# Attention and activation transposes on TensorE as pairs of bf16 in one 4-byte element

## What is computed

```
h = x @ W_in + b_in            -> q (1024) | k (256) | v (256) | z (2048) | gate_a (1024) | gate_g (1024)
y_a = attention(q, k, v, sinks) @ W_branch_attn     # 16 query heads, 4 key heads, head size 64, window 128
y_g = (u * (tril(W_s) LN(v') + b_s)) @ W_branch_gmlp, u | v' = gelu(z), chunks of 128 positions
mix = sigmoid(gate_a) * y_a + sigmoid(gate_g) * y_g
x1  = LayerNorm(alpha * x + mix @ W_out)
out = LayerNorm(alpha * x1 + relu(x1 @ W_up)^2 @ W_down)      # W_up 1024 x 4096
```

## Time and profile before

| | us |
|---|---|
| median of 3 runs (range) | 1052.94 (1052.09 to 1054.36) |
| the profiled execution, its own time | 1046.84 |
| its span, first to last instruction, slowest core | 1045.3 |
| TensorE busy in it | 1023.3 (98%) |
| DVE busy | 611.5 (59%) |
| ACT busy | 360.4 (34%) |
| POOL busy | 89.1 (9%) |

### The profile page before, as it was taken

One profiled execution on the slowest core, in us unless ns is written; L12 is line 12 of the kernel. 1 busy time (PEld: TensorE's weight loads), 2 busy tenths in 40 slices (PEclk: granted clock), 3 DMA queues, 4 the chain that ended last, 5 costly groups with the idle time before them and its releaser, 6 DMA issues.

```text
span 1045.3 us, 16998 instructions; the slowest of 8 cores (1043.9 to 1045.3 us)
## 1 busy us (share of the span) xinstructions
PE 1023.3 (98%) x6054; PEld 498.9 (48%) x6054; DVE 611.5 (59%) x1087; ACT 360.4 (34%) x484; POOL 89.1 (9%) x152
## 2 busy tenths in 40 slices
PE   8999999999999999999999999999999999999994
PEld 3446455554444444444444645555444444444442
DVE  2866477765876312336787827777486832133476
ACT  0454666651425200330024646666123430023100
POOL 4210000000111000000012000000010100010000
PEclk9999999999999999999999999999999999999998
DMA  9995234241797812953198222542156464086011
GB/s 160 188 174 95 41 53 98 54 102 33 150 162 150 142 20 35 166 82 82 61 185 149 50 41 44 91 102 51 61 124 138 75 129 80 1 134 108 21 61 80
DMA packets 20484, 98.65 MB, mean 94 GB/s; under 512 B 2353, under 2 KB 2993, under 8 KB 11954
## 3 DMA queue, kind: packets, MB, share of 16 engines
q0 software_dynamic: 13344, 73.41, 42.1%
q1 hardware_dynamic: 7058, 24.16, 6.8%
HBM read 162.57 MB, written 8.39 MB: 164 GB/s over the span
## 4 chain that ended last, share of the span: by engine, by line
PE 93%; DVE 3%; DMA 1%; issue 1%; ACT 1%; POOL 0%; DVEq 0%; POOLq 0%; ACTq 0%
PE ps L431 61%; PE ps L1147 20%; PE ps L924 3%; PE ps L674 2%; PE ps L942 2%; PE ps L889 2%; DMA ring<-wz 1%; PE ps L795 1%; DVE scr L392 1%; PE ps L972 1%; PE ps L1063 1%; PE ps L742 1%; DVE scr L897 0%; ACT scr L409 0%; DVE Cg L392 0%
## 5 line engine op out<-in xcount | busy, mean ns | idle before, releaser
L431 PE MATMUL ps<-reg,ring 128*128 128x512 bf16 x1536 | 344.7, 379 | 0.0
L431 PE MATMUL ps<-xT_s,ring 128*128 128x512 bf16 x1120 | 252.2, 375 | 0.2 <-DVE reg L392 0.2
L431 PEld LDWEIGHTS ps<-reg,ring 128*128 128x128 bf16 x1536 | 147.6, 98 | 172.7 <-issue 2.1
L1147 PE MATMUL ps<-ring,reg 128*128 128x512 bf16 x992 | 214.8, 379 | 0.0
L403 ACT ACTIVATE scr<-ps 128x512 f32<-128x512 f32 x128 | 76.4, 597 | 263.4 <-PE ps L431 260.0
L431 PEld LDWEIGHTS ps<-xT_s,ring 128*128 128x128 bf16 x1120 | 104.0, 98 | 115.0 <-issue 4.5
L392 DVE SCALAR_TENSOR_TENSOR reg<-ps,scr 128x512 bf16<-128x512 f32 x128 | 87.7, 690 | 113.8 <-ACT scr L403 113.7
L1147 PEld LDWEIGHTS ps<-ring,reg 128*128 128x128 bf16 x992 | 97.1, 98 | 117.0
L897 DVE CUSTOM_DVE_ANT_1 scr<-ps,masks 128x1024 f32<-128x1024 f32 x64 | 78.1, 1220 | 42.8 <-PE ps L889 34.9
L403 ACT ACTIVATE scr<-scr,amx 128x1024 bf16<-128x1024 f32 x64 | 73.2, 1144 | 15.9 <-DVE amx L392 11.8
L459 POOL DMA_DIRECT2D ring<-wst x62 | 34.6, 561 | 456.8 <-PE ps L431 165.2
(11 more groups left out here) (85 smaller groups left out, 722.7 us busy)
## 6 DMA issues: line engine op xcount, KB each, us to landing
ring<-wst POOLq DMA_DIRECT2D x62, 1024.0 KB, 10.7
regK<-x SPq DMA_DIRECT2D x16, 512.0 KB, 6.7
y<-scr SPq DMA_DIRECT2D x15, 512.0 KB, 2.6
lnbuf<-lnrep SPq DMA_DIRECT2D x4, 1024.0 KB
xT_s<-xt POOLq DMA_DIRECT2D x2, 1024.0 KB, 22.4
ring<-wz POOLq DMA_DIRECT2D x2, 1024.0 KB, 10.1
xT_s<-xt POOLq DMA_DIRECT2D x7, 256.0 KB, 19.3
ring<-wz POOLq DMA_DIRECT2D x7, 256.0 KB, 16.0
```

The costliest lines, as they stand in the source:

```text
L431: r = e.matmul(out, lhsT=a, rhs=b, start=(k == 0), stop=(k == 7))
L1147: r = e.matmul(ps[:, b2 + half, :], lhsT=hreg[fi // 8][:, th, fi % 8, bb * 128:(bb + 1) * 128], rhs=wd[quarter][:, fi % 4, half * 512:(hal ...
```

## The change

At all three places two bf16 neighbours are read as one float32, so that a row of 256 bf16 is 128 elements and one 128 x 128 transpose moves what two did: 4 transposes in place of 8, with a float32 identity. The bits pass through unchanged; in PSUM the two bf16 of a pair lie next to each other. The copy out of PSUM now reads every second bf16 and writes them side by side.

- Attention probabilities: Exp writes key s of half c at place 2s + c, so that the pair is (key s, key 128 + s), and the copy has the same order (j, c, q) in `pts` as before.
- Attention output and x1: the pair is two neighbouring features, 2p and 2p + 1, so partition p of the even block holds feature 2p of 256. The host orders the rows of W_branch_attn and W_up to match (`pairs`); their loads have the same shape and size.
- The identity is loaded straight into its own float32 buffer; its cast goes. The planner's figure for a transpose group is 0.23 in place of 0.45; that for Exp is written as 1.2 (1.19 by the helper's rule). The figures for the copies are as before.

```diff
-        identb = sb("identb", [128, 128], BF16)
+        ident = sb("ident32", [128, 128])
...
-            ld(idf, ident_d[:, :], [B_idf], after)
+            ld(ident[:], ident_d[:, :], [C["ident"]], after)
...
-            cp(identb[:], idf, [B_idf], [C["ident"]])
...
-                act(p16, ms, AF.Exp, bms + [B_amx[ai]], bpt, bias=mx[:, 4 + bb:5 + bb], scale=0.125)
+                act(p16.rearrange("p (j s c) -> p j c s", j=4, c=2), ms.rearrange("p (j c s) -> p j c s", j=4, c=2), AF.Exp, bms + [B_amx[ai]], bpt,
+                    bias=mx[:, 4 + bb:5 + bb], scale=0.125).cost = 1.2
...
                     for j in range(4):
                         pj = (j % 2) * 2 + j // 2
-                        for cc in range(2):
-                            r = e.transpose(out=PTp[:, j, cc, :], in_=c["p16"][:, pj * 256 + cc * 128:pj * 256 + (cc + 1) * 128], identity=identb[:])
+                        r = e.transpose(out=PT[:, j, :], in_=c["p32"][:, pj * 128:(pj + 1) * 128], identity=ident[:])
...
-                timed(P.op("pe", f, reads=c["bpt"] + [C["ident"]], writes=[B_ps[b]]), 0.45)
+                timed(P.op("pe", f, reads=c["bpt"] + [C["ident"]], writes=[B_ps[b]]), 0.23)
...
-                either(pts.bitcast(BF16), ps[:, b, :].bitcast(BF16), [B_ps[b]], bpts)
+                either(c["pts"], ps[:, b, :].bitcast(BF16).rearrange("p (j q c) -> p j c q", j=4, c=2), [B_ps[b]], bpts)
...
-                    for e2 in range(2):
-                        for b4 in range(4):
-                            r = e.transpose(out=AT[:, e2, b4 * 128:(b4 + 1) * 128], in_=ablk[:, bi, b4, e2 * 128:(e2 + 1) * 128], identity=identb[:])
+                    for b4 in range(4):
+                        r = e.transpose(out=ps[:, b, b4 * 128:(b4 + 1) * 128], in_=A32[:, b4 * 128:(b4 + 1) * 128], identity=ident[:])
...
-                either(attnT[:, th, 2 * hk:2 * hk + 2, :], AT, [B_ps[b]], [B_at[th]])
+                either(attnT[:, th, 2 * hk:2 * hk + 2, :], ps[:, b, :].bitcast(BF16).rearrange("p (t e) -> p e t", e=2), [B_ps[b]], [B_at[th]])
...
-                    for e_ in range(8):
-                        r = e.transpose(out=XT[:, e_, :], in_=xb[:, e_ * 128:(e_ + 1) * 128], identity=identb[:])
+                    for e2 in range(4):
+                        r = e.transpose(out=ps[:, b, e2 * 128:(e2 + 1) * 128], in_=xb[:, e2 * 128:(e2 + 1) * 128], identity=ident[:])
...
-                either(x1T[:, th, :, bb * 128:(bb + 1) * 128], XT, [B_ps[b]], [B_x1T[blk]])
+                either(x1T[:, th, :, bb * 128:(bb + 1) * 128].rearrange("p (f e) t -> p f e t", e=2),
+                       ps[:, b, :].bitcast(BF16).rearrange("p (f t e) -> p f e t", f=4, e=2), [B_ps[b]], [B_x1T[blk]])
...
+    def pairs(w):
+        return np.ascontiguousarray(np.transpose(w.reshape(-1, 128, 2, w.shape[1]), (0, 2, 1, 3)).reshape(w.shape))
+    w_up0, w_dn0, w_o0 = pairs(f(w_up)[0]), f(w_down)[0], f(w_out)[0]
+    wa0, wg0 = pairs(f(w_branch_attn)[0]), f(w_branch_gmlp)[0]
```

More of the change, by code:

```diff
@@ L557, in build_program @@
         ts(hgate[:], bcol[:, 16:32], 0.5, ALU.mult, [C["bcol"]], [C["hgate"]])
-        t01, t2, idf = r3f[:, 0:1024], r3f[:, 1024:1152], r3f[:, 1152:1280]
+        t01, t2 = r3f[:, 0:1024], r3f[:, 1024:1152]
         ones = r3f[:, 1280:1344].bitcast(BF16)
-        B_tri, B_idf = Buf("tri"), Buf("idf")
+        B_tri = Buf("tri")
         def load_consts(after):
@@ L808, in group @@
                 Prog.alias_after(B_ablk, [B_zero])
-                Prog.alias_after(B_at, [B_cst, B_tri, B_idf, C["ones"]])
+                Prog.alias_after(B_at, [B_cst, B_tri, C["ones"]])
             else:
@@ L904, in att_S @@
                 p16 = pt.bitcast(BF16)
-                act(p16, ms, AF.Exp, bms + [B_amx[ai]], bpt, bias=mx[:, 4 + bb:5 + bb], scale=0.125)
-                cx[t].update(p16=p16, bpt=bpt)
+                act(p16.rearrange("p (j s c) -> p j c s", j=4, c=2), ms.rearrange("p (j c s) -> p j c s", j=4, c=2), AF.Exp, bms + [B_amx[ai]], bpt,
+                    bias=mx[:, 4 + bb:5 + bb], scale=0.125).cost = 1.2
+                cx[t].update(p32=pt, bpt=bpt)
                 if bb == 3:
@@ L916, in att_T @@
                 b = 2 + rot("ptb", 2)
-                PTp = ps[:, b, :].bitcast(BF16).rearrange("p (j c q) -> p j c q", j=4, c=2)
+                PT = ps[:, b, :].rearrange("p (j q) -> p j q", j=4)
                 def f(e):
@@ L965, in att_A @@
                 b = 2 + rot("ptb", 2)
-                AT = ps[:, b, :].bitcast(BF16).rearrange("p (e q) -> p e q", e=2)
+                A32 = ablk[:, bi].rearrange("p b c -> p (b c)").bitcast(F32)
                 def f(e):
                     r = None
-                    for e2 in range(2):
-                        for b4 in range(4):
-                            r = e.transpose(out=AT[:, e2, b4 * 128:(b4 + 1) * 128], in_=ablk[:, bi, b4, e2 * 128:(e2 + 1) * 128], identity=identb[:])
-                    return r
-                timed(P.op("pe", f, reads=[B_ablk[bi], C["ident"]], writes=[B_ps[b]]), 0.45)
-                either(attnT[:, th, 2 * hk:2 * hk + 2, :], AT, [B_ps[b]], [B_at[th]])
+                    for b4 in range(4):
+                        r = e.transpose(out=ps[:, b, b4 * 128:(b4 + 1) * 128], in_=A32[:, b4 * 128:(b4 + 1) * 128], identity=ident[:])
+                    return r
+                timed(P.op("pe", f, reads=[B_ablk[bi], C["ident"]], writes=[B_ps[b]]), 0.23)
+                either(attnT[:, th, 2 * hk:2 * hk + 2, :], ps[:, b, :].bitcast(BF16).rearrange("p (t e) -> p e t", e=2), [B_ps[b]], [B_at[th]])
             SK = 5
@@ L1051, in o_K @@
                 either(xb.bitcast(BF16), x1[:, blk, :], [B_x1[blk]], bxb)
-                oc[blk] = (xb.bitcast(BF16), bxb)
+                oc[blk] = (xb, bxb)
             def o_C(blk):
@@ L1057, in o_C @@
                 b = bank()
-                XT = ps[:, b, :].bitcast(BF16).rearrange("p (e t) -> p e t", e=8)
                 def f(e):
                     r = None
-                    for e_ in range(8):
-                        r = e.transpose(out=XT[:, e_, :], in_=xb[:, e_ * 128:(e_ + 1) * 128], identity=identb[:])
-                    return r
-                timed(P.op("pe", f, reads=bxb + [C["ident"]], writes=[B_ps[b]]), 0.45)
-                either(x1T[:, th, :, bb * 128:(bb + 1) * 128], XT, [B_ps[b]], [B_x1T[blk]])
+                    for e2 in range(4):
+                        r = e.transpose(out=ps[:, b, e2 * 128:(e2 + 1) * 128], in_=xb[:, e2 * 128:(e2 + 1) * 128], identity=ident[:])
+                    return r
+                timed(P.op("pe", f, reads=bxb + [C["ident"]], writes=[B_ps[b]]), 0.23)
+                either(x1T[:, th, :, bb * 128:(bb + 1) * 128].rearrange("p (f e) t -> p f e t", e=2),
+                       ps[:, b, :].bitcast(BF16).rearrange("p (f t e) -> p f e t", f=4, e=2), [B_ps[b]], [B_x1T[blk]])
             B_hT = [[[Buf("hT") for _ in range(2)] for _ in range(16)] for _ in range(2)]
@@ L1270, in tile @@
         return np.transpose(w[:, c0:c0 + n].reshape(-1, 128, n), (1, 0, 2)).reshape(128, -1)
-    w_up0, w_dn0, w_o0 = f(w_up)[0], f(w_down)[0], f(w_out)[0]
-    wa0, wg0 = f(w_branch_attn)[0], f(w_branch_gmlp)[0]
+    def pairs(w):
+        return np.ascontiguousarray(np.transpose(w.reshape(-1, 128, 2, w.shape[1]), (0, 2, 1, 3)).reshape(w.shape))
+    w_up0, w_dn0, w_o0 = pairs(f(w_up)[0]), f(w_down)[0], f(w_out)[0]
+    wa0, wg0 = pairs(f(w_branch_attn)[0]), f(w_branch_gmlp)[0]
     def pieces(a):
```

## The result

The changed kernel is slower: 1058.88 us median (1058.37 to 1060.1) against 1052.51 in the same runs, ratio 1.0065 with a 95% interval of 1.0053 to 1.0078. Measured again in another set of runs it was 1054.08 against 1046.87, ratio 1.0072 (1.0059 to 1.0084). The forecast was 1049.8, faster.

A forecast was written before the change was run, and what follows sets the result against it. TensorE, busy 98%, was taken to bound the kernel. Transposes -4.6, DVE copies +1.5 and the rest 0 made -3.1 us, from 1052.94 to 1049.8; own range 1042 to 1056.5, with rivals 1031.4 to 1074.

The forecast's parts named there:

- Part 1: All transposes on TensorE: 96 groups of eight, each holding it 0.448 us, 43 us in all.
- Part 2: TensorE's transpose groups: four float32 transposes take 0.40 us against 0.448, over 96 groups -4.6 us.
- first line of that list: Transpose groups with load and stream both as in the float32 matmul rows: 0.428 us a group, -2 us.
- rival A: Transpose groups: float32 transposes go at bf16 pace, load and stream; -19 us, 1034; chance 0.30.
- Part 3, Exp at 0: Exp on ACT, writing with a step of 4 bytes, stays at 1144 ns: 0 us.
- Part 3, copies on DVE: 29 DVE copies go from 688 to 1225 ns, 15.6 us more of DVE; effect on time +1.5 us.
- cover of 2.6 us: In the attention, a copy ends 2.6 us before the product that reads it starts, so the copy stays covered.
- Part 4: Identity cast and load, weight row order and planner's order: 0 us, ends -4 and +4; engine shares shift by few copies.
- Rival B: All 96 groups: float32 load does not run ahead, or two instructions per transpose; 1074, or 1094 as pairs; chance 0.18.
- Rival C: DVE becomes the bound in the attention, the copies' 15.6 us come out whole; +11 us, 1064; chance 0.07.

The follow-up runs named there:

- The corner with both short: Same run as e4: changed kernel with Exp and the three copies both side by side; ratio 0.9996 to the kernel before.
- the probe: Rows of 16 equal TensorE operations on constants, ahead of the first attention stage of a kernel with bf16 probabilities; float32 transposes 0.11 us apart, bf16 0.06.
- e2: Changed kernel with the three copies out of PSUM reading side by side, Exp still writing every second place; ratio 1.0028 to the kernel before.
- e4: Changed kernel with both Exp and the three copies side by side, same operations and order; ratio 0.9996 to the kernel before.
- f1: Changed kernel with Exp side by side, the three copies still taking pairs apart; ratio 1.0043 to the kernel before.
- run 66: Not a follow-up run: part of "two engines that run 66 to 80% busy there", the busy share of DVE and ACT in the attention.
- f3: Changed kernel with the planner's figure for a transpose group put back from 0.23 to 0.45; ratio 1.0081 to the kernel before.
- e3: Changed kernel with the weaving moved from Exp to the score matmuls' PSUM write, masks laid out to match; ratio 1.0134 to the kernel before.
- e6: Changed kernel with the weaving moved from Exp to the scores' moving operand (K read woven), masks to match; ratio 1.0153 to the kernel before.

## Why the prediction was wrong

The direction was wrong: 3.1 us faster forecast, 6.4 to 7.2 slower measured. By its own steps:

- **Part 1** (the count, 43 us for 96 groups) held: 8 for 4 instructions, 0.45 us a group.
- **Part 2** (a float32 group at 0.40 us, -4.6) was mis-sized. A group behind a dense matmul is 0.437 us, near the first line of that list (0.428, -2), but the 34 groups behind a product with V are 0.467, longer than in bf16, and the sum of both is 0. The corner with both short measured -0.4 (-1.5 to +0.5). The reading behind it failed as well. I took the 0.11 us between two float32 loads for the load's pace and left the stream open; the probe has it the other way round, 0.107 for the stream of 128 columns and 0.067 or less for the load (of 64 rows). The row that would have told, the float32 stream at 0.84 ns a column, was there, and I moved away from it by an argument that no row carried (a transpose forms no product).
- The Trainium skill's "TensorE: Matmul & The Clock Gate", section "Terms", says that the transpose mode makes FP32 four times faster. Here a float32 transpose takes 0.107 us, and the float32 matmul two instructions of 0.84 ns a column, so 0.215 for 128. The factor is two, and rival A did not come. The Trainium skill's other rule on that page, section "Weight-path perf modes — Fast Weight Load (FWL) and DoubleRow", is that the fast weight load is not used for FP32. The trace agrees in that a load lasts 141 ns, 98 for bf16. In a row of transposes it is hidden; only behind the short matmuls of the product with V (0.03 us apart) are the groups longer, by 0.02 us, because the second of the four transposes starts 0.139 us after the first, not 0.109. That fits a load that could not run ahead; no run separates it.
- **Part 3, Exp at 0**, is a term put at nothing without a row. I bounded it by "a step of 4 bytes is what float32 has", read from ACT's reads, and gave its upper end no number. The two rows behind it, 512 float32 and 1024 bf16, differ in size and type at once, and neither writes with a step. Exp writes 1024 bf16 in 1437 ns in place of 1144, and that is +3.0 to +3.3 us, by e2 against e4 and the changed kernel against f1.
- **Part 3, copies on DVE**: the duration was right (1225 forecast, 1219 and 1223 measured). The Trainium skill's "VectorE: DVE Perf Modes", section "What auto-detection actually checks", wants step 1 for the doubled mode, and the trace agrees. Their effect, +1.5, was mis-sized threefold: +4.6 to +4.9. I counted 25 copies at one small wait each. There were 36, and with 19.3 us more in a list of DVE that already gates banks 0, 1 and 4 it is 0.13 us of time per copy, in this order. The cover of 2.6 us was real for the copy and not for the operations behind it.
- **Part 4, the order at 0** held: 0.9999 and 1.0081. That the planner's shares would shift "by a few copies at most" did not: 29 became 36.
- The terms with their measured sizes: -0.4 + 3.2 + 4.7 = 7.5 us, which is 0.0072 of 1046.9; the medians differ by 7.2. Against the forecast of -3.1 that is 10.6 us: 4.2 from Part 2, 3.2 from Exp and 3.2 from the copies. Any one of them by itself would have brought the sum to about 0 (+1.1, +0.1, +0.1); it took two of the three to make a clear loss.
- Rival B did not come (0.43 us a group, no load out of line). Rival C was the right mechanism, DVE in the attention, at 4.7 of the 15.6 us that it was priced at. No rival had ACT in it.

## What to carry to other kernels

Before a layout is packed for TensorE, price what ACT and DVE pay to weave and unweave it, each direction on each engine, and treat a duration that no row shows as a range, not as 0. Where TensorE is 98% busy, but in one stage waits now and then for chains on two engines that run 66 to 80% busy there (DVE 84.0 of 108 and 89.4 of 112 us, ACT 72.3 and 78.9, in the second measurement), a us added to these engines there cost 0.17 us (Exp, 3.2 of 18.8) to 0.24 us (copies, 4.7 of 19.3), though TensorE never waited for the lengthened copy. These two prices were measured in one order of instructions; f3, with fewer stretched copies on DVE and no smaller loss, shows that they need not carry over to another. And a saving on the first engine has to be larger than that: halving the instructions gave 0.01 us a group behind dense matmuls and cost 0.02 behind the product with V, because the time went by bytes.

## What the hardware showed that I had not expected

- A float32 transpose streams at 0.84 ns a column, a bf16 one at 0.44: equal bytes, equal time. In a row of them the weight load is not the pace.
- ACT's Exp of 1024 elements with bf16 written at every second place takes 1437 ns, with float32 read from alternate halves 1372, with neither 1144; its copies out of PSUM, which read bf16 at every second place, take 1017 to 1022 as without the step.
- A score matmul of 256 columns that writes float32 to every second place of PSUM, or whose moving operand jumps between two blocks of 128 keys, takes 402 and 406 ns, not 274, and four of them 0.54 and 0.59 us, not 0.32 (the four at 123.45 us in the changed kernel are followed at 123.77). The woven write first, from the chains of e3 and e6:

```profile
110.44 0.54 PE ps L888 x4
```

```profile
110.64 0.59 PE ps L888 x4
```

- A plain step of 2 in the moving operand costs 5% at 512 columns (10.6 ns) and 4% at 256 (0.114 for 0.110 us); in the weights nothing (64 column matmuls 0.03 us apart, with and without).
- A group of four float32 transposes takes 0.437 us behind a dense matmul and 0.467 behind the product with V; eight bf16 ones 0.447 and 0.446.
